# Gate and projection of the last two layers' embedding, interleaved by output tile into a second residual buffer, with the output stored in four pieces

## What is computed

```python
def second_block(x, p, ...):
    h = x
    for i in range(2):
        a = rmsnorm(h, norm_mix_pre[i])
        ...                                              # mixer
        h = h + rmsnorm(mix, norm_mix_post[i])
        m = rmsnorm(h, norm_mlp_pre[i])
        m = square(relu(m @ w_up[i])) @ w_down[i]
        h = h + rmsnorm(m, norm_mlp_post[i])
        gate = sigmoid(h @ ple_gate[i])                  # 1024 x 1024
        h = h + gate * (p[i] @ ple_proj[i])              # 256 x 1024
    return h
```

## Time and profile before

| | |
|---|---|
| median of 3 runs | 2184.2 us |
| lowest and highest run | 2176.87 and 2187.16 us |
| span of the profiled execution, first to last instruction | 2175.7 us |
| time of the profiled execution beyond its span | not listed on its own |
| TensorE busy | 2113.0 us, 97% |
| VectorE busy | 1256.1 us, 58% |
| ScalarE busy | 512.7 us, 24% |
| mean granted TensorE clock | 0.996 |

### The profile page before, as it was taken

The page is one execution under the profiler, slowest core; times in us unless marked ns, Lnnn a source line. Parts: engine busy times, 40 slices in busy tenths (PEclk is TensorE's granted clock), DMA queues, the critical chain, the costliest instruction groups (busy, mean ns, idle before and its releaser), DMA issues.

```text
span 2175.7 us, 34560 instructions
## 1 busy us (share of the span) xinstructions
PE 2113.0 (97%) x14648; PEld 1501.3 (69%) x14648; DVE 1256.1 (58%) x2173; ACT 512.7 (24%) x1064; POOL 188.2 (9%) x180
## 2 busy tenths in 40 slices
PE   7999999999999999999999999999999999999998
PEld 4446767464788885457466995686895488769646
DVE  2664444567754547652356775585786428678743
ACT  2434333351300000022162000223210122421101
POOL 0004333000000000002100000002121000202100
PEclk9999999999999999999999999999999999999999
DMA  8122354404422224445203444333444433334441
GB/s 355 58 77 77 121 196 177 146 2 193 155 97 78 97 78 155 174 140 131 78 2 119 173 174 174 131 118 118 148 175 174 156 134 116 117 135 169 169 176 68
DMA packets 41672, 289.94 MB, mean 133 GB/s; under 512 B 5040, under 2 KB 6448, under 8 KB 7216
## 3 DMA queue, kind: packets, MB, share of 16 engines
q1 hardware_dynamic: 39344, 279.99, 35.2%
q0 software_dynamic: 1312, 3.15, 1.1%
q10 hardware_dynamic: 864, 4.61, 0.5%
HBM read 286.15 MB, written 1.05 MB: 132 GB/s over the span
## 4 chain that ended last, share of the span: by engine, by line
PE 89%; DVE 5%; ACT 3%; issue 2%; DMA 1%; ACTq 0%; DVEq 0%
PE banks L1036 22%; PE banks L1564 14%; PE banks L1845 12%; PE banks L3036 6%; PE banks L2377 6%; PE banks L417 5%; PE banks L2057 2%; PE banks L644 2%; PE banks L816 1%; PE banks L3030 1%; PE banks L455 1%; PE banks L831 1%; PE banks L822 1%; PE banks L852 1%; PE banks L2015 1%
## 5 line engine op out<-in xcount | busy, mean ns | idle before, releaser
L1036 PE MATMUL banks<-arena 128*128 128x512 f32 x392 | 186.2, 593 | 0.7 <-DVE arena L1901 0.5
L1036 PE MATMUL banks<-weight_ring,arena 128*128 128x512 f32 x338 | 156.8, 593 | 0.0
L1036 PEld LDWEIGHTS banks<-arena 128*128 128x128 f32 x392 | 74.0, 190 | 93.8 <-issue 92.4
L1564 PE MATMUL banks<-normed,weight_ring 128*128 128x128 f32 x1040 | 130.8, 276 | 2.3 <-ACT normed L575 1.2
L3036 PE MATMUL banks<-normed,weight_ring 128*128 128x256 f32 x576 | 130.7, 387 | 1.2 <-DVE normed L561 0.6
L2377 PE MATMUL banks<-normed,weight_ring 128*128 128x512 f32 x288 | 126.1, 593 | 0.0
L1564 PEld LDWEIGHTS banks<-normed,weight_ring 128*128 128x128 f32 x1040 | 123.2, 192 | 3.7 <-issue 2.9
L3036 PEld LDWEIGHTS banks<-normed,weight_ring 128*128 128x128 f32 x576 | 110.9, 194 | 18.7 <-issue 2.5
L1001 DVE TENSOR_TENSOR arena<-weight_ring 128x512 f32<-128x512 f32 x67 | 46.2, 690 | 130.9 <-PE banks L1036 130.8
L1564 PE MATMUL banks<-normed,arena 128*128 128x128 f32 x960 | 116.4, 275 | 2.1 <-DVE arena L1530 2.1
L1036 PEld LDWEIGHTS banks<-weight_ring,arena 128*128 128x128 f32 x338 | 63.5, 190 | 76.5 <-issue 75.7
(11 more groups left out here) (500 smaller groups left out, 3868.2 us busy)
## 6 DMA issues: line engine op xcount, KB each, us to landing
weight_ring<-in_weights SPq DMA_DIRECT2D x266, 1024.0 KB, 4.8
residual<-in_tokens ACTq DMA_DIRECT2D x1, 2048.0 KB, 15.0
mix<-in_rpb POOLq DMA_DIRECT2D x32, 64.0 KB, 3.6
constants<-in_const ACTq DMA_DIRECT2D x1, 1953.5 KB, 11.1
out<-residual SPq DMA_DIRECT2D x1, 1024.0 KB, 4.8
branch<-arena POOLq DMA_DIRECT2D x1, 512.0 KB, 5.1
normed<-in_ple POOLq DMA_DIRECT2D x1, 512.0 KB, 3.4
vector_params<-in_vectors ACTq DMA_DIRECT2D x1, 223.0 KB, 5.7
```

The costliest lines, as they stand in the source:

```text
L1036: return pe.matmul(self.bank[i], left, b, start=(p == 0), stop=(p == n - 1))
L1564: mm = pe.matmul(o, a[:, k * P:k * P + P], right[:, k], start=(k == 0), stop=(k == H - 1))
```

## The change

The packing puts, for each output tile, its two projection blocks ahead of its eight gate blocks. One function, `embedding`, replaces both `matmul_stage` calls. On TensorE it runs for each `m` the projection and then the gate, in banks 6 and 7 for the projection and 0, 2 and 3 for the gate. It begins with `need(pe, deps)`, where `deps` is `r + [(p_ready, pb + 16)]`. ScalarE takes the gate out, VectorE multiplies and adds tile by tile. The sum goes into the other residual buffer, `y[:, :, S:]`, and after the layer `h`, `y` and `R.y` trade places. `root_table` stands behind the eight sigmoids. The output is stored in four transfers of two tiles each, each waiting for its second tile.

```diff
-        out.append(pack_tiles(x["ple_gate_2"][i], columns(D)))
-        out.append(pack_tiles(x["ple_proj_2"][i], columns(D)))
+        gate, proj = (pack_tiles(x[n][i], columns(D)).reshape(KT, -1, P, P) for n in ("ple_gate_2", "ple_proj_2"))
+        out.append(np.concatenate([proj, gate], 1).reshape(-1, P, P))
...
+def embedding(K, h, p, out, deps, k_ready):
+    made, taken, done = (K.counter(n) for n in ("products", "taken_out_by_scalar", "taken_out_by_vector"))
+    mb, tb, db = made.reserve(2 * KT), taken.reserve(KT), done.reserve(2 * KT)
+    gate_banks, product_banks = (0, 2, 3), (6, 7)
+    first = [K.next_blocks(KT + 2, (made, mb + 2 * m + 2)) for m in range(KT)]
+
+    def tensor(pe):
+        need(pe, deps)
+        for m in range(KT):
+            if m >= 2:
+                pe.wait_ge(done.sem, db + 2 * m - 3)
+            for k in range(2):
+                K.arrived(pe, first[m] + k)
+                mm = pe.matmul(K.bank(product_banks[m % 2], S), K.block(first[m] + k), p[:, k, :], start=(k == 0), stop=(k == 1))
+            mm.then_inc(made.sem, 1)
+            if m >= 3:
+                pe.wait_ge(taken.sem, tb + m - 2)
+            for k in range(KT):
+                if m == 0:
+                    need(pe, k_ready(k))
+                K.arrived(pe, first[m] + 2 + k)
+                mm = pe.matmul(K.bank(gate_banks[m % 3], S), K.block(first[m] + 2 + k), h[:, k, :], start=(k == 0), stop=(k == KT - 1))
+            mm.then_inc(made.sem, 1)
+
+    def scalar(act):
+        for m in range(KT):
+            act.wait_ge(made.sem, mb + 2 * m + 2)
+            act.activation(out[:, m, :], K.bank(gate_banks[m % 3], S), ACT.Sigmoid).then_inc(taken.sem, 1)
+
+    def vector(dve):
+        for m in range(KT):
+            dve.wait_ge(made.sem, mb + 2 * m + 1)
+            dve.wait_ge(taken.sem, tb + m + 1)
+            dve.tensor_tensor(out=out[:, m, :], in0=out[:, m, :], in1=K.bank(product_banks[m % 2], S), op=ALU.mult).then_inc(done.sem, 1)
+            dve.wait_ge(done.sem, db + 2 * m + 1)
+            dve.tensor_tensor(out=out[:, m, :], in0=out[:, m, :], in1=h[:, m, :], op=ALU.add).then_inc(done.sem, 1)
+
+    K.add(tensor=tensor, scalar=scalar, vector=vector)
+    root_table(K)
+    return [(done, db + 2 * KT)], lambda k: [(done, db + 2 * k + 2)]
...
-            r = matmul_stage(K, KT, KT, lambda k: lat[:, k, :], S, lambda e, m, ps: e.activation(y2[:, m, :], ps, ACT.Sigmoid), [], k_ready=tiles)
-
-            root_table(K)
-
-            def embed(dve, m, ps):
-                K.in_turn(dve, "vector")(dve.tensor_tensor(out=y2[:, m, :], in0=y2[:, m, :], in1=ps, op=ALU.mult))
-                return dve.tensor_tensor(out=lat[:, m, :], in0=lat[:, m, :], in1=y2[:, m, :], op=ALU.add)
...
-            r = matmul_stage(K, KT, 2, lambda k, layer=layer: pT[:, layer, k, :], S, embed, r + [(p_ready, pb + 16)], who=lambda m: "vector", banks=(0, 2, 3, 5))
+            r, tiles = embedding(K, h[:, :, S:], pT[:, layer], y[:, :, S:], r + [(p_ready, pb + 16)], tiles)
+            h, y, R.y = y, h, h.rearrange("p k n -> p (k n)")
...
-            need(sp, final)
-            sp.dma_start(out, lat).then_inc(stored.sem, 16)
-            sp.wait_ge(stored.sem, 16)
+            for k in range(0, KT, 2):
+                need(sp, tiles(k + 1))
+                sp.dma_start(out[:, k:k + 2, :], final[:, k:k + 2, :]).then_inc(stored.sem, 16)
+            sp.wait_ge(stored.sem, 16 * KT // 2)
```

More of the change, by code:

```diff
@@ L3463, in program @@
                 r, tiles = down.run(h, gain(layer, 3), r)
-        token_sums = [R.y[:, 512 * i:512 * i + 512].rearrange("p (k n) -> p k n", k=4) for i in range(4)]
-        lat = h[:, :, S:T2]
         pT = R.u[:, KT * S:KT * S + 4 * S].rearrange("p (l k n) -> p l k n", l=2, k=2)
@@ L3477, in program @@
         u2 = R.u[:, 0:KT * S].rearrange("p (k n) -> p k n", k=KT)
-        y2 = R.y[:, 0:KT * S].rearrange("p (k n) -> p k n", k=KT)
         R.mix2 = R.m[:, 0:KT * S].rearrange("p (k n) -> p k n", k=KT)
         for layer in range(2):
+            token_sums = [R.y[:, 512 * i:512 * i + 512].rearrange("p (k n) -> p k n", k=4) for i in range(4)]
+            token_y = R.y[:, 0:4 * 512].rearrange("p (q n) -> p q n", q=4)
             def plain(name, layer=layer):
@@ L3494, in program @@
             r, tiles = down.run(h, plain("norm_mlp_post"), r)
-            r = matmul_stage(K, KT, KT, lambda k: lat[:, k, :], S, lambda e, m, ps: e.activation(y2[:, m, :], ps, ACT.Sigmoid), [], k_ready=tiles)
-            root_table(K)
-            def embed(dve, m, ps):
-                K.in_turn(dve, "vector")(dve.tensor_tensor(out=y2[:, m, :], in0=y2[:, m, :], in1=ps, op=ALU.mult))
-                return dve.tensor_tensor(out=lat[:, m, :], in0=lat[:, m, :], in1=y2[:, m, :], op=ALU.add)
-            embedded = K.counter("taken_out_by_vector")
-            tiles = lambda k, base=embedded.n: [(embedded, base + k + 1)]
-            r = matmul_stage(K, KT, 2, lambda k, layer=layer: pT[:, layer, k, :], S, embed, r + [(p_ready, pb + 16)], who=lambda m: "vector", banks=(0, 2, 3, 5))
+            r, tiles = embedding(K, h[:, :, S:], pT[:, layer], y[:, :, S:], r + [(p_ready, pb + 16)], tiles)
+            h, y, R.y = y, h, h.rearrange("p k n -> p (k n)")
         stored = K.counter("stored")
-        final = r
+        final = h[:, :, S:]
         def store(sp):
-            need(sp, final)
-            sp.dma_start(out, lat).then_inc(stored.sem, 16)
-            sp.wait_ge(stored.sem, 16)
+            for k in range(0, KT, 2):
+                need(sp, tiles(k + 1))
+                sp.dma_start(out[:, k:k + 2, :], final[:, k:k + 2, :]).then_inc(stored.sem, 16)
+            sp.wait_ge(stored.sem, 16 * KT // 2)
         assert K.taken == n_blocks, (K.taken, n_blocks)
```

## The result

The changed kernel takes 2185.73 us (median of 20 runs, 2178.25 to 2193.46). The kernel before takes 2179.03 us (median of 20, 2175.09 to 2187.16). The ratio is 1.003, 95% interval 1.0019 to 1.0041: 4.1 to 8.9 us slower, +6.7 us by the medians. That is within 0.5%. The forecast was +4.9 us. The forecast's 2189.1 us is 3.4 us too high because the three runs that it started from had their median (2184.2) 5.2 us above that of the twenty; the shift itself was too small by 1.8 us.

The account below looks back on a forecast made before the run. TensorE, busy for 2113.0 of 2175.7 us, was taken to bound the kernel. Layer 0's +4.7 us and layer 1's +0.2 gave +4.9, carried from a median of 2184.2 to 2189.1 us, range 2182 to 2197.

Parts of the forecast that it names:

- Head: Start of the embedding: TensorE's first matmul waits for all eight residual tiles, +2.73 us.
- Matmuls and the hop: Embedding loop: 160 matmuls per layer still take 34.8 us; the projection's 0.46 us wait for the last sigmoid goes.
- Tail: Layer 0 behind the last gate matmul: sigmoid, table load, tiny root and eight squares in series on ScalarE, +2.65 us.
- T: The time at which TensorE's last embedding matmul ends; forecast at 1777.4 in layer 0, where it was 1775.42.
- Second buffer, ring: Writing the sum to the other residual buffer, and freeing the embedding's weight chunks later: no cost.
- Store: End of layer 1: the last of four output pieces lands in about 2.55 us instead of 4.8.
- Sum: Whole kernel: 4.7 us for layer 0 and 0.2 for layer 1, +4.9 us.
- the squares hide after all: Rival, layer 0 behind the last matmul: squares run ahead of the last sigmoid; +0.9 us, 2185.1 us, chance 0.04.
- The clock: Rival: TensorE's new idle stretches make the granted clock fall, 1.7 us per fall; +13.1 us together, 2197.3 us, chance 0.07.

Follow-up runs that it names:

- filled kernels: Unused matmuls in TensorE's idle stretches: in the changed kernel, ratio 1.0006; behind the last gate, with head waiting only for p and squares between sigmoids, 0.9972 (both against before).

## Why the prediction was right

*Head.* Predicted +2.73 us: TensorE at 0.04 us behind the end of L1136. It starts at 1747.80, 3.28 us behind the start of L1136 where it was 0.54: +2.74. Shown from both sides, by taking the wait away and by putting it in.

*Matmuls and the hop.* Predicted 34.8 us for 160 matmuls. From 1747.80 to 1782.62 are 34.82 us; the waits inside cost nothing. The net delay of the end of the last matmul against the start of L1136 was to be +2.0 us and is 38.10 - 36.08 = +2.02.

*Tail.* Predicted: first square at T + 1.92, large root at T + 6.26, so +2.65 us. Measured: 1784.45 is T + 1.83, the root T + 6.16, so +2.55. The table load followed the sigmoid directly and was followed directly. The drain of 1.38 us in the Trainium skill ("ScalarE: Activation LUTs", "What ACT_TABLE_LOAD costs") shows in neither this kernel nor the one without the tiny root; the load's 1.28 us does.

*Second buffer, ring.* Predicted nothing. VectorE's operations take 0.42 us in either buffer, and TensorE has no gap in the loop.

*Store.* Predicted 2.55 us for the last piece; the profile's page has 2.5 as the median of the four. Layer 1 was to cost +0.2 us and costs +0.2.

*Sum.* 4.7 + 0.2 = 4.9 predicted, 4.56 + 0.2 = 4.8 measured in the stretches. The median alone would not have told: 2185.7 us lies nearer to the 2185.1 of the rival "the squares hide after all" than to the forecast's 2189.1, only because the base was too high; the rows between T and the root decide. What missed is outside of the stretches: the base (the median of three runs), and 1.3 us between the stretches (+4.8) and the mean of all runs (+6.1), which is less than the uncertainty of 1.5.

*The clock.* I gave it a chance of 0.07 as a case that either comes with all its price or does not. It comes by execution. Seven profiles have the unfilled wait at the head, in two layers each: in 2 of these 14 stretches the clock fell, at 1.7 us each, as priced. In the 12 such stretches of the six profiles without that wait, or with it filled, it never fell; numbers this small can also come by chance. By that count the changed kernel pays 2 x 2/14 x 1.7 = 0.5 us on average at its heads. That is an upper estimate, as one of the two falls had another missing behind it. Part of the missing 1.3 us may be that; the runs do not prove it. Behind its tail, in five profiles with 2.3 us of idle TensorE, it never fell. That the price fits is partly luck. It was taken from slow matmuls at the start of the kernel, where the windows list the clock as 1.00, and with a distance of 0.25 us between matmuls; with the gate's 0.217 the same rows give 2.2 us.

*Left open.* Whether the unused matmuls are what lifts the mean clock of the filled kernels to 0.9966 and 0.9967, above the kernel before (0.9951), which has no such idle stretch, and if so where. Their single profiles have five and three falls, and the kernel before has five; no profile here isolates the cause.

## What to carry to other kernels

When two stages are merged, look at what each engine's list has behind the last item. Here the short stage at the end had been hiding the table load and the early squares, and the merge put the engine with the longest list of leftover work last. A wait that was per tile must stay per tile: moving "all of `r`" to the head cost 2.7 us per layer, more than the 0.46 us hop that the merge removed. The split store is worth its 2.3 us alone; try such parts one by one. And read on behind the stretch that an edit shortens: a fall of the clock can move from one stretch into another, and is then no cost of the edit.

## What the runs showed of the hardware

An execution's time follows the granted clock: over the changed kernel's first 20 runs the span and the mean clock have a correlation of -0.94, from 2176.2 us at 0.998 to 2191.7 at 0.991. Read in windows of 5 us, every loss of clock in the 13 profiles is 1.7 us or twice that, and at the places looked at in windows of 1 us the granted clock goes down to 0.50, that is 1.2 GHz. The places recur; what differs from execution to execution is which of them are hit, and whether once or twice. One is hit in all 13 profiles, between 1405 and 1420 us, for 1.7 us in eight of them and 3.4 in five. What TensorE does just ahead of it is this, shown at its second occurrence, in layer 0 of the kernel before, where the clock falls between 1798 and 1800 us:

```profile
1794.48 3.64 PE L3030 MATMUL banks<-weight_ring,normed 128*128 128x16 f32 x32
```

These are 32 matmuls of 16 columns without idle time: TensorE counts as busy, and the clock falls all the same in 13 of 13 profiles at the first place and in 9 of 13 at the second. So idle time is not all that precedes a fall.

The falls make a spread of 15 us in a kernel that does the same work each time, so a change of 5 us is read from landmarks, and from twenty runs or more, not from one span. The Trainium skill says of this gate that activity releases the throttle ("TensorE: Matmul & The Clock Gate", "What's actually happening"); the trace agrees in that two of the falls came right behind 2.66 us in which TensorE waited, and three more behind 5 us in which it was busy for less than 4. The falls behind L3030, where it never waited, are not explained by waiting.
